# Paged decode attention in a fused decoder layer: keys turned by VectorE, four 32-column float32 tiles on TensorE, pages laid on 32 partitions

## The reference, cut to what matters

```python
# q: (B, Tq, H, 2, 64); k segments: cache (B, 2048, H, 2, 64) and new keys; v: (B, Tk, H, 128)
s = jnp.einsum('bqhcd,bkhcd->bhcqk', q, k) * 64 ** -0.5      # causal mask on the new keys
p = jax.nn.softmax(jnp.concatenate(scores, axis=-1), axis=-1)
w = p[:, :, 0] - lam * p[:, :, 1]
out = sum(jnp.einsum('bhqk,bkhe->bqhe', w_seg, v_seg))
o = rms_norm(out, g) * (1 - lambda_init)
```

## Time and profile before

| what | us |
|---|---|
| median of 3 runs (lowest to highest) | 1790.78 (1787.35 to 1791.5) |
| the profiled execution's own time | 1784.04 |
| its span, first to last instruction | 1782.2 |
| sample attention, first page turned to the GLU products | 324.5 to 611.7 |
| one turn of its loop | 34.3 |

### The profile page before, as it was taken

One profiled execution on the slowest core, in us unless ns is written; L12 is line 12 of the kernel. 1 busy time (PEld: TensorE's weight loads), 2 busy tenths in 40 slices (PEclk: granted clock), 3 DMA queues, 4 the chain that ended last, 5 costly groups with the idle time before them and its releaser, 6 DMA issues.

```text
span 1782.2 us, 21928 instructions
## 1 busy us (share of the span) xinstructions
PE 1493.8 (84%) x6889; PEld 687.5 (39%) x6889; DVE 624.6 (35%) x1247; ACT 369.5 (21%) x707; POOL 88.3 (5%) x154
## 2 busy tenths in 40 slices
PE   3989756688888798899998999999998999999870
PEld 2537534566676463433332222222232222222220
DVE  1366786688788622511111111111111111111104
ACT  1104223477677501100000000000000000000001
POOL 0000001011001000000000000000000000000003
PEclk7999876789889899799999999999999999999995
DMA  9220024377876823499999999999999999999974
GB/s 387 73 95 1 0 82 154 113 248 247 254 239 197 330 83 115 191 384 419 417 419 417 420 416 419 417 419 419 417 420 416 419 416 420 418 419 418 416 325 138
DMA packets 128560, 535.59 MB, mean 301 GB/s; under 512 B 20625, under 2 KB 21362, under 8 KB 92658
## 3 DMA queue, kind: packets, MB, share of 16 engines
q1 hardware_dynamic: 106914, 493.00, 69.8%
q0 software_dynamic: 10896, 35.27, 5.6%
q10 hardware_dynamic: 10720, 6.95, 1.3%
HBM read 519.30 MB, written 15.88 MB: 300 GB/s over the span
## 4 chain that ended last, share of the span: by engine, by line
SPq 41%; PE 32%; DVE 13%; issue 6%; DMA 4%; ACT 2%; ACTq 0%; DVEq 0%; POOLq 0%; POOL 0%
PE psum L887 27%; SPq L487 23%; SPq L485 18%; PE psum L890 5%; DMA ring<-in_w_in 2%; DMA ring<-in_w_down 2%; DVE keys_low L1585 1%; DVE values_low L1589 1%; DVE ring L1596 1%; DVE ring L1471 1%; DVE arena L1847 1%; DVE ring L1472 1%; DMA ring<-expert_rows,rowi 0%; ACTq L640 0%; DVE ring L1449 0%
## 5 line engine op out<-in xcount | busy, mean ns | idle before, releaser
L887 PE MATMUL psum<-ring,arena 128*64 128x512 f32 (+3 forms) x3472 | 861.3, 597 | 83.0 <-DMA ring<-in_w_down 49.0
L887 PEld LDWEIGHTS psum<-ring,arena 128*64 128x64 f32 (+2 forms) x3472 | 263.3, 140 | 641.2 <-issue 397.0
L887 PE MATMUL psum<-arena 128*64 128x512 f32 (+5 forms) x972 | 242.3, 578 | 45.2 <-ACT ring L608 30.2
L1789 DVE TENSOR_SCALAR arena<-psum 128x512 f32<-128x512 f32 x33 | 22.8, 692 | 392.1 <-PE psum L887 392.1
L887 PEld LDWEIGHTS psum<-arena 128*64 128x64 f32 (+2 forms) x972 | 93.8, 162 | 170.1 <-issue 115.4
L887 PE MATMUL psum<-arena,ring 128*128 128x288 f32 x480 | 128.0, 429 | 14.6 <-DMA ring<-in_w_in 9.0
L770 ACT ACTIVATE arena<-psum 128x512 f32<-128x512 f32 x34 | 20.4, 599 | 515.9 <-PE psum L887 515.9
L890 PE MATMUL psum<-cst,ring 128*128 128x128 f32 (+1 forms) x640 | 93.3, 296 | 35.2 <-DVE keys_low L1585 21.5
L887 PEld LDWEIGHTS psum<-arena,ring 128*128 128x128 f32 x480 | 95.8, 202 | 45.6 <-DMA ring<-in_w_in 13.0
L1804 DVE COPY arena<-psum 128x512 f32<-128x512 f32 x33 | 22.8, 692 | 241.7 <-PE psum L887 241.7
L890 PE MATMUL psum<-cst,arena 128*128 128x128 f32 (+2 forms) x455 | 67.4, 285 | 40.2 <-DVE arena L1326 15.3
(11 more groups left out here) (249 smaller groups left out, 935.8 us busy)
## 6 DMA issues: line engine op xcount, KB each, us to landing
ring<-in_w_gate_up SPq DMA_DIRECT2D x264, 1024.0 KB, 20.9
ring<-in_w_down SPq DMA_DIRECT2D x132, 1024.0 KB, 25.2
ring<-in_cache_k SPq DMA_DIRECT2D x128, 256.0 KB, 3.0
ring<-in_cache_v POOLq DMA_DIRECT2D x64, 256.0 KB, 4.2
ring<-in_cache_v SPq DMA_DIRECT2D x64, 256.0 KB, 3.0
expert_rows<-arena POOLq DMA_DIRECT2D x66, 128.0 KB, 5.5
ring<-in_w_in SPq DMA_DIRECT2D x8, 1024.0 KB, 23.5
ring<-in_w_gate SPq DMA_DIRECT2D x8, 1024.0 KB, 21.4
```

The costliest lines, as they stand in the source:

```text
L887: return nc.tensor.matmul(out, lhsT=a, rhs=b, start=start, stop=stop, skip_group_check=True)
L1789: TS(gg, gate_half, LIMIT, None, ALU.min).then_inc(e_g, 1)
```

## The change

The sample attention is written anew, in float32 without a split into high and low parts.

- **Layout.** A page is laid on 32 partitions (32j to 32j+31 for page j of its slot), four successive keys (8 KB) in each. All key DMAs stay on SP, whose queue now holds only keys there; all value DMAs are issued by POOL.
- **Keys.** One VectorE transpose in 32x32 blocks turns a whole slot (128 x 2048) into slots 8 to 11, which hold the turned keys of one batch. These blocks put 32 components of a head on each group of partitions beside four groups of pages, so the stationary queries (`Qs`) are a block pattern of 32 columns that keeps the four groups apart: 4 groups x 8 rows. Scores of head h go to partitions 32h to 32h+31, four matmuls (e) for each head, each of 512 columns: four column tiles of 32.
- **Softmax** stands on 128 partitions x 512. The maximum and the sum over the four groups are combined by small VectorE transposes and one matmul with `sameq`. Normalising, the factor with lambda, and the sum of the two components are one product with the matrix `Dg`; a VectorE transpose turns the weights.
- **Values.** 16 matmuls of 512 columns, in four column tiles, one for each group of partitions' page; `sample_place` puts the rows of a batch into place and `sample_add` sums them.
- **Order.** Batches are unrolled. TensorE: weights of b, scores of b+1, values of b, placing of b. VectorE turns the slots of b+1 between the steps of b. The first score needs `sample_prepare` (queries copied to four groups, turned, and put into `Qs`).
- **Ring.** `w_glu`, `w_bs0`, `w_bs1`, `w_ba0` come into slots 0 to 3 behind the last keys, `w_ba1` and `w_out0` to `w_out2` into 8 to 11, `w_out3` into 4. The constants are 302 columns wider; the last tile of rows is cleared once (128 x 512), and four turns of sample queries and keys by TensorE are gone. The norm of the sample heads works on 128 x 128 instead of 32 x 512.

```diff
-RING += [(f"K{s}", s, 4, NB) for s in range(4)] + [(f"V{s}", 4 + s, 0 if s in V_BY_POOL else 4, NB) for s in range(4)]
-RING += [("w_glu", 8, 1, 1), ("w_bs0", 9, 1, 1), ("w_bs1", 10, 1, 1), ("w_ba0", 11, 1, 1), ("w_ba1", 0, 1, 1)]
-RING += [(f"w_out{k}", 1 + k, 1, 1) for k in range(4)]
+RING += [(f"K{s}", s, 4, NB) for s in range(4)] + [(f"V{s}", 4 + s, 0, NB) for s in range(4)]
+RING += [(f"KT{s}", 8 + s, 0, 1) for s in range(4)]
+RING += [("w_glu", 0, 1, 1), ("w_bs0", 1, 1, 1), ("w_bs1", 2, 1, 1), ("w_ba0", 3, 1, 1), ("w_ba1", 8, 1, 1)]
+RING += [(f"w_out{k}", (9, 10, 11, 4)[k], 1, 1) for k in range(4)]
...
-FIRST_SLOT = 5
+CHUNK_SLOTS = (5, 6, 7, 0, 1, 2, 3, 8, 9, 10, 11, 4)
...
+        KT = ring[:, 8:12, :].rearrange("p s (g c i) -> p (s g) c i", g=4, c=16)
+        QT = at(6912, H, 4, NB, NS)
+        knT = at(7424, 16, NSMP)
+        Qs = at(I0, NB, H, 4, 32)
+        E = at(I0 + 4096, 544)
+        wT = at(I0 + 4640, NPG, 32)
+        wTn = at(I0 + 5152, 32)
+        Osb = at(I0 + 5184, 512)
+        snw = at(I0 + 5696, 32)
+        Dg = at(I0 + 5728, KVQ, 32)
+        mcol, mturn, mback, nbias = (at(I0 + 5856 + 32 * i, 32) for i in range(4))
+        osum = at(I0 + 5984, DV)
...
-                    eng.dma_start(ring[:, SLOT[name], j * 512:(j + 1) * 512],
-                                  cache[ds(page, 1), :, :].rearrange("o p n -> p (o n)")).then_inc(
+                    eng.dma_start(ring[32 * j:32 * j + 32, SLOT[name], :],
+                                  cache[ds(page, 1), :, :].rearrange("o (p r) n -> p (o r n)", r=4)).then_inc(
...
+            with sp.Fori(1, NB) as b:
+                pages_of(sp, "K", ck, b)
...
-            sp.wait_ge(s_s5, 1)
-            with sp.Fori(0, NB - 1) as b:
-                pages_of(sp, "K", ck, b + 1, (0, 1, 2))
-                pages_of(sp, "V", cv, b, V_BY_SP)
-                pages_of(sp, "K", ck, b + 1, (3,))
-            pages_of(sp, "V", cv, NB - 1, V_BY_SP)
-            sp.wait_ge(s_eT, NB)
...
+            def sample_exps(b):
+                act.wait_ge(k_nbias, b + 1)
+                nc.scalar.activation(E[:, 512:544], snw, ACT.Exp, scale=SCALE, bias=nbias[:, 0:1], accum_out=es[:, 1:2])
+                nc.scalar.activation(E[:, 0:512], psum[:, 4 * (b % 2), :], ACT.Exp, scale=SCALE, bias=nbias[:, 0:1],
+                                     accum_out=es[:, 0:1]).then_inc(k_exp, 1)
+            def sample_pv_copy(b):
+                act.wait_ge(k_pv, b + 1)
+                if b:
+                    act.wait_ge(k_ot, b)
+                nc.scalar.activation(Osb, psum[:, 2, :], ACT.Copy).then_inc(k_o, 1)
+            for b in range(NB):
+                sample_exps(b)
+                sample_pv_copy(b)
+            head_rms(2, P, 1)
...
-                pages_of(pool, "V", cv, j, V_BY_POOL)
+                pages_of(pool, "V", cv, j)
...
+            def queries_copy():
+                pe.wait_ge(s_kvtok, 1)
+                for a in range(KVQ):
+                    last = mm(M2[0][32 * a:32 * a + 32, :], ident[0:NSMP, 0:NSMP], qk[0:NSMP, 0, 2, :], True, True)
+                last.then_inc(k_rep, 1)
+            def sample_scores(b):
+                for s in range(4):
+                    pe.wait_ge(freed[SLOT[f"K{s}"]], free_at(f"K{s}", b + 1))
+                S, M = S2[b % 2], M2[b % 2]
+                if b > 1:
+                    pe.wait_ge(k_acc, b - 1)
+                for e in range(4):
+                    for h in range(H):
+                        mm(S[32 * h:32 * h + 32, :], Qs[:, b, h, e, :], KT[:, :, 4 * h + e, :], e == 0, e == 3)
+                for e in range(4):
+                    for h in range(H):
+                        last = mm(M[32 * h:32 * h + 32, 0:NSMP], Qs[:, b, h, e, :], knT[:, 4 * h + e, :], e == 0, e == 3)
+                        if b == NB - 1 and e == 3 and h == H - 1:
+                            last.then_inc(k_scored, 1)
+                if b < NB - 1:
+                    last.then_inc(k_scored, 1)
+            def sample_weights(b):
+                pe.wait_ge(k_etot, b + 1)
+                M = M2[b % 2]
+                    last = mm(M[32 * h:32 * h + 32, 32:33], C("sameq")[:, 32 * h:32 * h + 32], etot, True, True)
+                last.then_inc(k_den, 1)
+                pe.wait_ge(k_dg, b + 1)
+                for a in range(KVQ):
+                    mm(W[32 * a:32 * a + 32, :], Dg[:, a, :], E[:, 0:512], True, True)
+                mm(M[0:32, 64:96], Dg[:, 0, :], E[:, 512:544], True, True).then_inc(k_w, 1)
+            def sample_values(b):
+                pe.wait_ge(k_wt, b + 1)
+                if b:
+                    pe.wait_ge(k_o, b)
+                for pg in range(NPG):
+                    s, g = pg // 4, pg % 4
+                    if g == 0:
+                        pe.wait_ge(s_vpool[s], 64 * (b + 1))
+                    last = mm(O[32 * g:32 * g + 32, :], wT[:, pg, :], ring[:, SLOT[f"V{s}"], g * 512:(g + 1) * 512],
+                              s == 0, s == 3 and g > 0)
+                    if g == 3:
+                        last.then_inc(freed[SLOT[f"V{s}"]], 1)
+                mm(O[0:32, :], wTn, vt[:, 2, :], False, True).then_inc(k_pv, 1)
+            def sample_place(b):
+                pe.wait_ge(k_o, b + 1)
+                M = M2[b % 2]
+                place = C("place").rearrange("p (h c) -> p h c", h=H)
+                    last = mm(M[32 * h:32 * h + 32, 128:256], place[:, h, 28 - NS * b:60 - NS * b], Osb[:, h * DV:(h + 1) * DV], True, True)
+                last.then_inc(k_ot, 1)
+            queries_copy()
+            pe.wait_ge(k_prep, 1)
+            sample_scores(0)
+            for b in range(NB):
+                sample_weights(b)
+                if b + 1 < NB:
+                    sample_scores(b + 1)
+                sample_values(b)
+                sample_place(b)
+            pe.wait_ge(k_acc, NB)
+            for s in range(4):
+                pe.sem_inc(freed[SLOT[f"KT{s}"]], 1)
...
+            def sample_prepare():
+                for c in (mcol, wTn):
+                    nc.vector.memset(c, 0.0)
+                nc.vector.memset(knT, 0.0)
+                step(nc.vector.memset(Qs, 0.0))
+                step(TT(sgn, sc[:, 11:12], C("second"), ALU.mult))
+                step(TT(sgn, sgn, C("first"), ALU.add))
+                nc.vector.transpose(knT[0:NSMP].rearrange("p c t -> p (c t)"), qk[0:NSMP, 1, 2, :])
+                v.wait_ge(k_rep, 1)
+                step(nc.vector.transpose(QT.rearrange("p h e b q -> p (h e b q)"), M2[0]))
+                for a in range(KVQ):
+                    rows_ = slice(32 * a, 32 * a + 32)
+                    for e in range(4):
+                        o = a * QC + e // 2 * NS
+                        ins = CP(Qs[rows_, :, :, e, o:o + NS], QT[rows_, :, e, :, :].rearrange("p h b q -> p b h q"))
+                ins.then_inc(k_prep, 1)
+            def turn_keys(b, s):
+                wait_loaded(v, f"K{s}", b)
+                if b:
+                    v.wait_ge(k_scored, b)
+                else:
+                    v.wait_ge(freed[SLOT[f"KT{s}"]], USE0[f"KT{s}"])
+                nc.vector.transpose(ring[:, SLOT[f"KT{s}"], :], slot(f"K{s}")).then_inc(freed[SLOT[f"K{s}"]], 1)
+            def sample_max(b):
+                v.wait_ge(k_scored, b + 1)
+                S, M = S2[b % 2], M2[b % 2]
+                nc.vector.tensor_reduce(m2[:, 0:1], S, AX.X, ALU.max)
+                step(TT(snw, M[:, 0:NSMP], C("newmask")[:, NSMP - NS - NS * b:2 * NSMP - NS - NS * b], ALU.add))
+                step(nc.vector.tensor_reduce(m2[:, 1:2], snw, AX.X, ALU.max))
+                step(TT(mcol[:, 0:1], m2[:, 0:1], m2[:, 1:2], ALU.max))
+                step(nc.vector.transpose(mturn, mcol))
+                step(nc.vector.tensor_reduce(m8, mturn.rearrange("p (a r) -> p r a", a=KVQ), AX.X, ALU.max))
+                step(TS(mback.rearrange("p (a r) -> p a r", a=KVQ), m8.unsqueeze(1).to_broadcast([P, KVQ, QC]), -SCALE, None, ALU.mult))
+                nc.vector.transpose(nbias, mback).then_inc(k_nbias, 1)
+            def sample_norm(b):
+                v.wait_ge(k_exp, b + 1)
+                M = M2[b % 2]
+                TT(etot, es[:, 0:1], es[:, 1:2], ALU.add).then_inc(k_etot, 1)
+                v.wait_ge(k_den, b + 1)
+                step(nc.vector.reciprocal(rden, M[:, 32:33]))
+                TS(Dg, C("pattern").rearrange("p (a c) -> p a c", a=KVQ), rden, sgn, ALU.mult, ALU.mult).then_inc(k_dg, 1)
+            def sample_turn(b):
+                v.wait_ge(k_w, b + 1)
+                if b:
+                    v.wait_ge(k_pv, b)
+                nc.vector.transpose(wTn[0:32, :], M2[b % 2][0:32, 64:96])
+                nc.vector.transpose(wT.rearrange("p g c -> p (g c)"), W).then_inc(k_wt, 1)
+            def sample_add(b):
+                v.wait_ge(k_ot, b + 1)
+                M = M2[b % 2]
+                if b == 0:
+                    CP(osum, M[:, 128:256]).then_inc(k_acc, 1)
+                else:
```

(20 more changed lines are left out.)

370 lines of the change are left out of this document (56 added, 314 removed).

## The result

The changed kernel takes 1802.1 us (1799.6 to 1805.7), against 1789.1 for the kernel before in the same rounds: a ratio of 1.0074, 95% interval 1.005 to 1.0098. It is slower by 0.7%, a small loss that the interval keeps apart from none, where I had forecast 1750 us and faster. The profiled execution spans 1803.6 us, 21.4 more than before.

The account below looks back on a forecast made before the run. No engine alone bounds the old loop; three hand pages to one another. Start, two 22.5 us periods, five DMA-limited 28.8 us periods and a tail save a net 41 us: 1743, forecast 1750 with the run offset; own range 1735 to 1775.

Parts of the forecast that it names:

- What bounds, and what saves comes through whole: Sample attention, 289.6 us up to the GLU products, is replaced; experts behind stay at 418 GB/s, so its saving carries through.
- Start, turn, scores: Before the loop: preparation 9.7 us to 331.8, 2.3 us a slot's turn, scores 7.1 us, first ready at 348.1.
- the scan's price: Dear bound for VectorE's transpose of one slot: 4.5 us, against the 2.3 us taken.
- The third rival: Compute price: turns at 4.5 us, or column tiles one after another, period about 40 us, 1850 us; chance 0.10.
- The loop of the engines: Per batch, VectorE's 13.8 us and the scores' 7.1 us follow one another: 20.9 us.
- GpSimd's pace: Value page issues on POOL, 1.22 us each, with slot waits and landing, set 22.5 us a batch where DMA is no limit.
- the first rival: Full DMA rate in the batch loop: seven periods of 22.5 us, net -74.6, 1716 us; chance 0.25.
- DMA: Page loads on 32 partitions: 20.1 us a batch at full rate, 37.4 at 224 GB/s; 28.8 taken.
- The middle: Batch period of 28.8 us, taken between 20.1 and 37.4 because the key and value queues are not coupled.
- five periods: The loop's later batches, after the two loaded ahead, at 28.8 us each: 144 us.
- tail to the GLU products: Behind the last scores: 29 us for last values, copy, placing and adding, 2 beside merge weights, smaller terms +2.5.
- The second rival: Both page queues on the same half, with gaps: middle period 42.7 us, net +28, 1818 us; chance 0.23.

Follow-up runs that it names:

- page_on_32_spread: Against the changed kernel, each page lies on every fourth partition instead of 32 neighbours, packets unchanged; 1708.2 us, 0.9571 of the kernel before.
- page_on_128: Against the changed kernel, each page is laid on 128 partitions again, one 2 KB key in each; 1709.3 us, 0.9549 of the kernel before.
- halves_alternate: Against the changed kernel, pages are issued 0,2,1,3 for keys and 2,0,3,1 for values, still on 32 partitions; 1785.3 us, 0.9986 of the kernel before.

## Why the prediction was wrong, step by step

**What bounds, and what saves comes through whole.** The loop as the place to price, the experts at 418 GB/s before and after: right for the experts. But 21.4 us were lost and only 13.5 of them ahead of the GLU products. Behind these, before took 1170.5 us to the end of the span, the change 1178.4, and the other kernels with all their expert jobs between 1170.0 and 1177.2. In the change the 96 matmuls that follow the merge weights took 43.27 us at a granted clock of 0.96, against 41.57 at 1.00; page_on_32_spread has the 43.27 too. The rest lies among later loads and clocks; no run was made for it, and the cause is open. A forecast from the stretch alone has an uncertainty of some 8 us that mine left out.

**Start, turn, scores: right in the sum, the scores partly by luck.** VectorE's preparation ended at 328.8 (forecast 331.8). A turn took 2276 ns where I had 2.3 us from the two-input step, so the scan's price is out. The scores (timeline of TensorE, start us, us):

```profile
337.84 6.03 PE L814 MATMUL psum<-ring,arena 128*32 128x512 f32 x32 [23.17 <-DVE ring L1490]
343.69 0.48 PE L814 MATMUL psum<-arena 128*32 128x32 f32 x32
...
362.11 3.64 PE L814 MATMUL psum<-ring,arena 128*32 128x512 f32 x32
```

They took 6.3 us in all against 7.1, and two errors met in that: the 16 matmuls over the cached keys took 5.9 us, where I had 3.5 and 1.4 for the clock, and the new keys 0.5, where I had 2.2. The granted clock was 0.62 in this stretch. The last row is 16 matmuls of the same form at a granted clock of 1.00, products with the values, in 3.64 us: one after another they would have taken 13.9, so four column tiles do run side by side. In the loop, where the clock is 0.60, scores take 5.3 to 6.4 us from their start to the reduction. First scores at 344.2, forecast 348.1. The third rival, compute price, falls.

**The loop of the engines: right within its use.** 20.9 forecast; 18.1 with everything loaded ahead, 20.4 with keys alone. **GpSimd's pace: near, not confirmed.** 22.5 forecast; by its own terms, 25.1 less half of the 3 us between the release of V0 and the last quarter, it would have been 23.6. The last five periods of page_on_128 have a mean of 24.3, those of page_on_32_spread, with the same issues, 22.1; taking half of the issues away from GpSimd in the right place brought 21.8 and 21.1. So the issues cost something, but as the layouts differ by as much, they don't set the period by themselves. The forecast of the first rival, 1716 us, is page_on_128 to within 7 us.

**DMA: the step that failed.** I wrote: "With keys on one half while values are on the other, the full rate should come back. The two queues are not coupled, so I take the middle of 20.1 and 37.4, 28.8 us". The upper bound was the answer: 38.9 us, 216 GB/s, where the earlier trace rows had given 224. The row had priced the half well, reads from SBUF standing for writes: it holds two transfers one after another, from partitions 0 to 63 and from 64 to 127, at 218 and 238 GB/s each. What was wrong was the escape from it, and it had no row: no trace showed two queues adding up. The middle needed 35% more than the measured rate (38.9 / 28.8); halves_alternate tried to bring it about and got 5.6% in its stretch and 7% in its period. A middle between two bounds that differ by a mechanism is a forecast that neither mechanism makes.

The sum against the trace:

| term | forecast | measured |
|---|---|---|
| first scores | 348.1 | 344.2 |
| two first periods | 45.0 | 44.5 |
| five periods | 144.0 | 194.5 |
| tail to the GLU products | 31 + 2.5 | 42.0 |
| GLU start | 570.6 | 625.2 |

50.5 of the 54.6 us are the five periods. The tail, 8.5, is the same error: it had the last value page 4.1 us after GpSimd's last issue, and in the chain it takes 15.7 and lands at 603.90 + 15.68 = 619.6, 36.3 us behind the last scores. With page_on_128 the tail is 32.1.

**The second rival** is what happened: the two queues share the rate of a half, a period above 37 decides. I had given it a chance of 0.23, against 0.42 for the middle. Its price, 42.7 for gaps between transfers, was too high (and its +28 makes 1819 from 1790.8, not 1818): the share stays at 1.02, there are no gaps, since the pages stand queued for 20 us and more before they land, which covers every wait for a slot. At its bound without gaps, 37.4, I had written "no change", net +2. Against that sum the five periods add 7.5 us and the tail 8.5, the start gives back 4.4, and the stage behind adds 8: about the 21.4 of the spans.

## What to carry to other kernels

Before a transfer's layout is changed, look which partitions one transfer reaches, not only how large its packets are: with each page within partitions 0 to 63 or 64 to 127, 16 engines at a share near 1 moved 214 to 256 GB/s, across both halves 365 to 395, with the same bytes, and in page_on_32_spread with the same packets. Where a rate is shared, don't count on queues falling apart, and don't average over two mechanisms; price each and choose. DMA issues cost their engine's stream (0.95 us each here on ScalarE, with the reading of the page number): put them where the engine waits anyway, behind the work that others wait for.

## What the runs showed of the hardware that I had not expected

- The DMA share doesn't tell a full rate from half of one. It is 1.02 at 214 GB/s and 1.02 at 418: both columns must be read.
- Within one half the layout still counts somewhat: neighbours 214, every second partition 243, 64 neighbours 256 GB/s. All three have both queues busy; why they differ is open.
- Packets of 2 KB on all partitions did about as well as packets of 8 KB on every fourth: 389 and 395 GB/s with three queues, 365 and 383 with two, and the same total each time.
- halves_alternate scattered over 26 us in ten executions (1771.6 to 1797.8), where page_on_128 had 4 in four and the change 6 in four. A fixed page order doesn't fix how the queues meet.
- Eight DMA issues on ScalarE took 7.58 us, 0.95 each, and the exponentials behind them waited. GpSimd's stand 1.22 apart in the kernel before and in page_on_128 alike.
